# Attention heads taken in pairs on the two halves of TensorE, in a two-block model kernel

## The reference

```
def stick_breaking(q, k, v):          # 8 heads, strictly causal
        z = jnp.einsum('bhqd,bhsd->bhqs', qi, kt) * scale
        log_beta = jax.nn.log_sigmoid(z)
        log_stay = jnp.where(mask, log_beta - z, 0.0)
        log_w = log_beta + lax.cumsum(log_stay, axis=3, reverse=True) - log_stay
        w = jnp.where(mask, jnp.exp(log_w), 0.0)
        return jnp.einsum('bhqs,bhsd->bhqd', w, vt)

def retention(q, k, v, positions):    # 8 heads; q and k turned by rotary()
    scores = jnp.einsum('bnihd,bnjhd->bnhij', qc, kc) * decay_intra
    y_intra = jnp.einsum('bnhij,bnjhd->bnihd', scores, vc)
    ...
```

## Time and profile before

| | us |
|---|---|
| median of 3 runs | 1219.01 (1217.12 to 1223.62) |
| the profiled execution's own time | 1221.8 |
| its span | 1219.7 |
| PE busy | 1046.9 (86%) |
| DVE busy | 887.2 (73%) |
| ACT busy | 438.0 (36%) |
| mean granted clock of TensorE | 0.944 of 2.4 GHz |

### The profile page before, as it was taken

How to read it: one execution, slowest core, us unless ns; L and a number is a source line. 1 busy time by engine, 2 the same in 40 slices (tenths; PEclk the granted TensorE clock), 3 DMA queues, 4 the chain that set the end, 5 groups by cost and what they waited for, 6 DMA issues and landing times.

```text
span 1219.7 us, 14397 instructions
## 1 busy us (share of the span) xinstructions
PE 1046.9 (86%) x5140; PEld 727.9 (60%) x5140; DVE 887.2 (73%) x1809; ACT 438.0 (36%) x845; POOL 291.8 (24%) x260
## 2 busy tenths in 40 slices
PE   6999989999989999976989977876687779766987
PEld 6988989999988776974655532332333334322343
DVE  6977679998768774588676877667766776677545
ACT  5646454444365544543232322222212221222112
POOL 0000000000000000013424644443444444434530
PEclk9999999999999999997999989988988899889999
DMA  9432459889808322029999999999999999999995
GB/s 361 179 139 87 139 211 353 317 326 333 290 35 310 114 94 69 2 102 372 419 419 373 422 421 420 422 421 421 421 422 422 420 422 420 422 421 422 422 421 209
DMA packets 67750, 378.59 MB, mean 310 GB/s; under 512 B 7520, under 2 KB 7776, under 8 KB 34912
## 3 DMA queue, kind: packets, MB, share of 16 engines
q0 software_dynamic: 36864, 268.45, 53.1%
q1 hardware_dynamic: 29952, 107.13, 24.1%
q10 hardware_dynamic: 864, 2.10, 0.5%
HBM read 376.61 MB, written 1.05 MB: 310 GB/s over the span
## 4 chain that ended last, share of the span: by engine, by line
PE 34%; DVE 29%; DMA 24%; ACT 7%; issue 5%; POOL 1%; SPq 0%; ACTq 0%; DVEq 0%
DMA ring_sb<-in_peer,idsb 16%; PE pb L839 5%; PE pb L412 5%; PE pb L415 5%; DVE ring_lo L1311 5%; PE pb L842 5%; DMA whi_rows<-in_peer,idsb 4%; PE pb L440 3%; DVE ring_sb L1840 3%; DMA arena<-in_peer,idsb 3%; DVE arena L1579 2%; DMA xn<-in_peer,idsb 2%; ACT whi L878 2%; DVE arena L1783 1%; DVE arena L1778 1%
## 5 line engine op out<-in xcount | busy, mean ns | idle before, releaser
L1903 POOL DMA_INDIRECT ring_sb<-in_peer,idsb x143 | 163.8, 1146 | 743.3 <-DVE idsb L1823 545.0
L412 PE MATMUL pb<-xhi,whi 128*128 128x256 f32 x928 | 241.7, 294 | 5.9 <-ACT whi L878 1.5
L415 PE MATMUL pb<-xlo,whi 128*128 128x256 f32 x928 | 235.2, 287 | 0.9 <-DVE xlo L1753 0.3
L1840 DVE CUSTOM_DVE_ANT_0 ring_sb<-ring_sb,arena 128x1024 f32<-128x1024 f32 x143 | 171.9, 1222 | 83.6 <-DMA ring_sb<-in_peer,idsb 83.6
L839 PE MATMUL pb<-ring_sb,arena 128*128 128x512 f32 x286 | 162.9, 653 | 81.0 <-ACT arena L1252 81.0
L412 PEld LDWEIGHTS pb<-xhi,whi 128*128 128x128 f32 x928 | 179.5, 193 | 12.8 <-issue 9.5
L415 PEld LDWEIGHTS pb<-xlo,whi 128*128 128x128 f32 x928 | 179.4, 193 | 6.6 <-issue 3.9
L1311 DVE TENSOR_TENSOR ring_lo<-ring_sb,whi 128x1024 fp32r<-128x1024 f32 x138 | 161.5, 1219 | 24.5 <-ACT whi L878 24.5
L1247 ACT ACTIVATE arena<-arena 128x4 f32<-128x4 f32 (+1 forms) x70 | 14.4, 205 | 414.5 <-DVE arena L1840 414.5
L842 PE MATMUL pb<-ring_sb,arena 128*128 128x512 f32 x286 | 156.6, 631 | 0.0
L839 PEld LDWEIGHTS pb<-ring_sb,arena 128*128 128x128 f32 x286 | 57.4, 209 | 157.2 <-issue 157.2
(11 more groups left out here) (320 smaller groups left out, 1646.0 us busy)
## 6 DMA issues: line engine op xcount, KB each, us to landing
ring_sb<-in_ada SPq DMA_DIRECT2D x48, 512.0 KB, 5.4
ring_sb<-in_w_gu SPq DMA_DIRECT2D x44, 512.0 KB, 6.7
ring_sb<-in_w_in SPq DMA_DIRECT2D x40, 512.0 KB, 7.5
ring_sb<-in_w_down SPq DMA_DIRECT2D x22, 512.0 KB, 5.8
ring_sb<-in_w_out SPq DMA_DIRECT2D x16, 512.0 KB, 3.5
ring_sb<-in_w_q SPq DMA_DIRECT2D x16, 512.0 KB, 6.2
ring_sb<-in_peer,idsb POOLq DMA_INDIRECT x143, 22.5
ring_sb<-in_w_iv SPq DMA_DIRECT2D x4, 512.0 KB, 15.9
```

Of the source, the lines that this page charges most:

```text
L412: e.matmul(o, hi_w(u)[:, c], xh(k), start=start, stop=False, skip_group_check=skip)
L415: e.matmul(o, hi_w(u)[:, c], xl(k), start=False, stop=False, skip_group_check=skip)
L1840: e.tensor_tensor_reduce(o, o, h2t[tile], 1.0, 0.0, MUL, ADD, aa[:, col:col + 1]).then_inc(*VD.up(("dot", col)))
L1903: e.indirect_dma_start(rows_at[s], None, peer, bass.IndirectOffsetOnAxis(ap=idsb[:, col:col + 1], axis=0)).then_inc(s_row[s], 16)
```

## The change

Heads are taken in pairs. `pair_scores` issues the 256-column product of both heads of a pair, then the 128-column product of both, each into a bank of its own; `pair_out` does the same with the outputs, both heads into one bank, in its two halves of partitions. The pairs stand in gaps between whole pairs of units: `sb_pair(h)` gives the outputs of heads h-4 and h-3, the cumulations of h-2 and h-1 and the logits of h and h+1. Four gaps hold what nine held; the gaps in the middle of the projections rq and rk for heads are gone. `az`, `be` and `st` exist 4 times. The ring of banks has 6 places during this stage and 4 again behind it. ACT and DVE work pair by pair as well. In the retention the scores of heads 0 to 3 stand together, then those of 4 to 7. The number of arithmetic instructions is the same.

```
-        az, be, st = ([arena[:, w9 + (3 * a + i) * 384:w9 + (3 * a + i + 1) * 384] for i in range(3)] for a in range(3))
+        az, be, st = ([arena[:, w9 + (4 * a + i) * 384:w9 + (4 * a + i + 1) * 384] for i in range(4)] for a in range(3))
...
-            ring[0] = [0, 1, 2, 3]
+            ring[0] = [0, 1, 2, 3, 4, 5]
...
-            def head_scores(kT, qT, h, name, until):
-                r, j = 64 * (h % 2), h // 2
-                b = bank(until)
-                where[name] = b
-                e.matmul(pb[b][:, 0:T], kT[r:r + 64, j * T:j * T + 128], qT[r:r + 64, j * T:(j + 1) * T], start=True, stop=True)
-                return e.matmul(pb[b][:, T:T + 128], kT[r:r + 64, j * T + 128:(j + 1) * T], qT[r:r + 64, j * T + 128:(j + 1) * T],
-                                start=True, stop=True)
-
-            def head_out(w, v, h, b):
-                r, o = 64 * (h % 2), (h // 2 % 2) * T
-                e.matmul(pb[b][r:r + 64, o:o + T], v[:, h * 64:(h + 1) * 64], w[:, 0:T], start=True, stop=False, skip_group_check=True)
-                return e.matmul(pb[b][r:r + 64, o + 128:o + T], v[:, 512 + h * 64:512 + (h + 1) * 64], w[:, T:T + 128],
-                                start=False, stop=True, skip_group_check=True)
+            def pair_scores(kT, qT, h, name, st_, until):
+
+                both, j = (h, h + 1), h // 2
+                for g in both:
+                    where[name, g] = bank((st_, (until, g)))
+                for g in both:
+                    r = 64 * (g % 2)
+                    e.matmul(pb[where[name, g]][:, 0:T], kT[r:r + 64, j * T:j * T + 128], qT[r:r + 64, j * T:(j + 1) * T],
+                             start=True, stop=True)
+                return [e.matmul(pb[where[name, g]][:, T:T + 128], kT[64 * (g % 2):64 * (g % 2) + 64, j * T + 128:(j + 1) * T],
+                                 qT[64 * (g % 2):64 * (g % 2) + 64, j * T + 128:(j + 1) * T], start=True, stop=True) for g in both]
+
+            def pair_out(ws, v, h, b):
+
+                o = (h // 2 % 2) * T
+                for i, w in enumerate(ws):
+                    e.matmul(pb[b][64 * i:64 * i + 64, o:o + T], v[:, (h + i) * 64:(h + i + 1) * 64], w[:, 0:T], start=True, stop=False,
+                             skip_group_check=True)
+                return [e.matmul(pb[b][64 * i:64 * i + 64, o + 128:o + T], v[:, 512 + (h + i) * 64:512 + (h + i + 1) * 64], w[:, T:T + 128],
+                                 start=False, stop=True, skip_group_check=True) for i, w in enumerate(ws)]
...
+            def sb_pair(h):
+
+                if h >= 4:
+                    sb_out(h - 4)
+                if 2 <= h <= 8:
+                    sb_weights(h - 2)
+                    sb_weights(h - 1)
+                if h < 8:
+                    sb_logits(h)
...
-            sb_step(0)
-            gemm(U_rq[0:2], ("rq", 0), (AR, ("rq", "raw", 0)), mid=lambda: sb_step(1))
-            sb_step(2)
+            sb_pair(0)
+            gemm(U_rq[0:2], ("rq", 0), (AR, ("rq", "raw", 0)))
+            sb_pair(2)
             gemm(U_rq[2:4], ("rq", 1), (AR, ("rq", "raw", 1)), mid=lambda: rope_turn("rq", 0))
-            sb_step(3)
+            sb_pair(4)
             rope_turn("rq", 1)
-            gemm(U_rk[0:2], ("rk", 0), (AR, ("rk", "raw", 0)), mid=lambda: sb_step(4))
-            sb_step(5)
+            gemm(U_rk[0:2], ("rk", 0), (AR, ("rk", "raw", 0)))
+            sb_pair(6)
             gemm(U_rk[2:4], ("rk", 1), (AR, ("rk", "raw", 1)), mid=lambda: rope_turn("rk", 0))
-            sb_step(6)
+            sb_pair(8)
             rope_turn("rk", 1)
-            sb_step(7)
-            gemm_tok(U_rv, "rv", (AR, "rv"), mid=lambda: sb_step(8))
-            sb_step(9)
+            gemm_tok(U_rv, "rv", (AR, "rv"), mid=lambda: sb_pair(10))
+            ring[0] = [0, 1, 2, 3]
...
-            for h in range(4):
-                ret_scores(h)
-                if h:
-                    ret_out(h - 1)
-                if h == 2:
-                    group_sum(AS, ("o", 0), AS, half(tmp, 0))
+            ret_scores(0)
+            ret_scores(2)
+            group_sum(AS, ("o", 0), AS, half(tmp, 0))
+            ret_out(0)
             gemm(U_rg[0:2], ("rg", 0), (AR, ("rg", 0)), mid=lambda: group_sum(AS, ("o", 1), AS, half(tmp, 1)))
-            for h in range(4, 8):
-                ret_scores(h)
-                ret_out(h - 1)
-                if h == 5:
-                    ret_mean(0)
-            ret_out(7)
+            ret_out(2)
+            ret_scores(4)
+            ret_scores(6)
+            ret_mean(0)
+            ret_out(4)
+            ret_out(6)
...
+            def sb_pair(h):
+                if 2 <= h <= 8:
+                    for g in (h - 2, h - 1):
+                        e.wait_ge(*VS.at(("be2", g)))
+                        e.activation(az[g % 4], be[g % 4], ACT.Exp).then_inc(*AS.up(("w", g)))
+                if h >= 8:
+                    return
+                for g in (h, h + 1):
+                    e.wait_ge(*PS.at(("z", g)))
+                    if h == 0:
+                        e.wait_ge(*VM.at(("red", 1)))
+                    if g >= 4:
+                        e.wait_ge(*PS.at(("out", g - 4)))
+                    e.activation(az[g % 4], pb[where["z", g]][:, 0:384], ACT.Abs, scale=0.125).then_inc(*AS.up(("abs", g)))
+                for g in (h, h + 1):
+                    e.wait_ge(*AS.at(("abs", g)))
+                    e.activation(az[g % 4], az[g % 4], ACT.Exp, scale=-1.0).then_inc(*AS.up(("exp", g)))
+                for g in (h, h + 1):
+                    e.wait_ge(*AS.at(("exp", g)))
+                    e.activation(az[g % 4], az[g % 4], ACT.Ln, bias=c_("one")).then_inc(*AS.up(("ln", g)))
...
+                for g in (h, h + 1):
+                    e.wait_ge(*PS.at(("cum", g)))
+                    e.tensor_tensor(be[g % 4], be[g % 4], pb[where["cum", g]][:, 0:384], ADD).then_inc(*VS.up(("be2", g)))
+
+            def sb_masks(h):
+                for g in (h, h + 1):
+                    e.wait_ge(*AS.at(("w", g)))
+                    e.tensor_tensor(diag(az[g % 4]), diag(az[g % 4]), sbm, MUL).then_inc(*VS.up(("w", g)))
+
+            def sb_pair(h):
+                if 2 <= h <= 8:
+                    sb_weights(h - 2)
+                    sb_masks(h - 2)
+                if h >= 8:
+                    return
+                for g in (h, h + 1):
+                    p = pb[where["z", g]][:, 0:384]
+                    e.wait_ge(*AS.at(("abs", g)))
+                    if g >= 4:
+                        e.wait_ge(*AS.at(("w", g - 4)))
+                    e.tensor_scalar(be[g % 4], p, 0.125, 0.0, MUL, MIN).then_inc(*VS.up(("be0", g)))
+                for g in (h, h + 1):
+                    m, p = g % 4, pb[where["z", g]][:, 0:384]
+                    e.wait_ge(*VS.at(("be0", g)))
+                    e.wait_ge(*AS.at(("ln", g)))
+                    e.tensor_tensor(be[m], be[m], az[m], SUB).then_inc(*VS.up(("be1", g)))
+                    e.wait_ge(*VS.at(("be1", g)))
+                    if g >= 4:
+                        e.wait_ge(*PS.at(("cum", g - 4)))
+                    e.scalar_tensor_tensor(out=st[m], in0=p, scalar=-0.125, in1=be[m], op0=MUL, op1=ADD).then_inc(*VS.up(("st0", g)))
+                    e.wait_ge(*VS.at(("st0", g)))
+                    e.tensor_tensor(diag(st[m]), diag(st[m]), sbm, MUL).then_inc(*VS.up(("st", g)))
```

More of the change, by code:

```diff
@@ L690, in sb_logits @@
                     e.wait_ge(*VS.at(("k", 1)))
-                head_scores(sbk, sbq, h, ("z", h), (VS, ("st0", h))).then_inc(*PS.up(("z", h)))
+                for g, mm in zip((h, h + 1), pair_scores(sbk, sbq, h, "z", VS, "st0")):
+                    mm.then_inc(*PS.up(("z", g)))
             def sb_weights(h):
-                n = h % 3
+                n = h % 4
                 b = bank((VS, ("be2", h)))
@@ L708, in sb_out @@
                 e.wait_ge(*VS.at(("w", h)))
[L709 to L717, removed]
+                e.wait_ge(*VS.at(("w", h + 1)))
+                for g, mm in zip((h, h + 1), pair_out([az[h % 4], az[(h + 1) % 4]], sv, h, 6 + h // 4)):
+                    mm.then_inc(*PS.up(("out", g)))
+            def sb_pair(h):
[6 more added lines that the diff above has]
+                    sb_logits(h)
             def rope_turn(name, i):
@@ L750, in ret_scores @@
                         e.wait_ge(*VR.at(("rk", "out", i)))
-                head_scores(rk2, rq2, h, ("rs", h), (VR, ("sc", h))).then_inc(*PR.up(("rs", h)))
+                for g, mm in zip((h, h + 1), pair_scores(rk2, rq2, h, "rs", VR, "sc")):
+                    mm.then_inc(*PR.up(("rs", g)))
             def ret_out(h):
@@ L759, in ret_out @@
                 e.wait_ge(*VR.at(("sc", h)))
-                head_out(scR[h % 4], rv, h, 4 + h // 4).then_inc(*PR.up(("out", h)))
+                e.wait_ge(*VR.at(("sc", h + 1)))
+                for g, mm in zip((h, h + 1), pair_out([scR[h % 4], scR[(h + 1) % 4]], rv, h, 4 + h // 4)):
```

(56 more changed lines are left out.)

26 lines of the change are left out of this document (removed).

## The result

| | before | changed | ratio, 95% interval |
|---|---|---|---|
| median, seven runs of each | 1219.01 us (1217.12 to 1223.62) | 1206.93 us (1202.25 to 1210.53) | 0.9885 (0.9861 to 0.991) |
| the same, compared again (before 11 runs, changed 6) | 1221.17 us (1217.0 to 1222.91) | 1205.31 us (1203.24 to 1208.72) | 0.9875 (0.9856 to 0.9894) |

The change saves 1.15%, 12.1 us between the medians, and 15.9 us in the second comparison. The forecast was 1206.6 us in a range of 1203.0 to 1213.5: right. Some terms of its sum are off all the same, and partly offset each other; the experiments are about them.

A forecast was written before the change was run, and what follows sets the result against it. PE was taken to bound stick-breaking and retention. Savings of 8.4 and 4.0 us sum to 12.4, taking the median from 1219.0 to 1206.6 us; the range was 1203 to 1210, or 1203 to 1213.5 with rivals 1 and 2.

The forecast's parts named there:

- PE bounds both stretches: Stick-breaking and retention: PE busy 60.6 of 62.5 and 22.5 of 24.1 us, so savings there count one for one.
- Row halves: Logits or scores of two heads overlap on PE's row halves: 0.87 a pair instead of 1.70, 3.3 us less in stick-breaking.
- Column halves: Two heads' outputs overlap fully on PE's column halves: 0.81 a pair, 3.1 us less in stick-breaking, 3.1 in retention.
- The fold: Eight 24-column matmuls on column quarters, all within 0.28 us, at least 0.33 one after another; evidence that columns overlap.
- rival 1: Column halves do not overlap; stick-breaking saves 3.1 less, total gain 7.8, 1211.2 us; chance 0.20.
- The walk through stick-breaking: PE's steps from first logits to rv's end: 8.6 less, including 1.9 of PE idling; 8.4 after a bank wait.
- The bank ahead of rk's second pair: DVE's turn of q's second half frees it at 430.1, PE asks at 430.0; put at 0.2 us.
- Slack of ACT and DVE: Second heads' masked logits in stick-breaking are ready before PE's cumulation asks; slack shrinks to 0.7 us.
- Rivals 2 and 3: 2: ACT or DVE bound last two pairs, gain 9, 1210, chance 0.15; 3: late chains lower PE's clock, 1225.4, 0.03.
- The ring of six: In force from some 50 us before 399; listed waits there not for banks, so 0, bounds minus 0.5 to plus 0.5.
- The walk through the retention: PE's steps from rv's end to the last mean: 20.05 instead of 24.1 us, saving 4.0 of the possible 5.6.
- All that follows is shifted: Work behind the attention starts earlier by what is saved; rest of the span stays 734 us, within 2 us.

The follow-up runs named there:

- the copy on DVE: Changed kernel with one more 128x1024 DVE copy, its result unused, behind each of the four pairs' logits; 1212.96 us (1 run).
- the same half: Changed kernel with both heads' outputs of a pair written to one half of PE's columns; 1207.49 us, ratio to before 0.989.
- heads apart: Changed kernel with stick-breaking work inside each gap taken head by head, retention as changed; 1214.10 us, ratio to before 0.9944.
- the turn on DVE first: Changed kernel with retention reordered to fill waits, and DVE's turn of q's second half ahead of rk's units' rest; 1205.36 us, ratio to before 0.9879.

## Why the prediction was right, point by point

- **PE bounds both stretches.** Right for stick-breaking: 52.74 of 53.12 us busy, and the copy on DVE shows that DVE is as close there as the prediction feared: 1.81 of 2.07 us added ahead of the bank came through. In the retention it holds only in part: 3.4 of 20.4 us are waits.
- **Row halves, 0.87 a pair.** Measured 0.85.
- **Column halves, 0.81 a pair, the nearer end of bounds 0.81 and 1.58.** Measured 0.80; 1.44 with the same half. The fold was the right row to judge by, and rival 1 is refuted. Its price of 3.1 for stick-breaking is that of both effects together, 4 x 0.78; the halves alone are worth 4 x 0.64, of which 2.1 came through (the wait at the bank covered 0.44), and 1.25 in the retention.
- **The walk through stick-breaking, saved 8.4.** S fell by 9.47. The retention's scores start 52.98 behind the first logits, where 53.9 was given (54.1 with the bank's 0.2, which that figure leaves out). The mis-sized term is two cumulations at 2 x 1.06: the four lots took 1.83, 1.93, 1.93 and 1.84, 0.95 less than 8.48 in all. 1.06 is the time of one that stands between two products on halves of the array; with whole-array work on both sides it is 0.87 (404.15 to 405.02), with it on one side 0.96 (405.02 to 405.98, or 402.36 to 403.32 with heads apart). Side by side, a pair has two such borders or one, where two single ones had four.
- **The bank ahead of rk's second pair, 0.2.** 0.38 idle; the turn on DVE first takes 0.44 off S.
- **Slack of ACT and DVE.** DVE ends the second heads' masks earlier than carried through. From DVE's timeline of the changed kernel:

```profile
412.48 0.42 DVE L1677 TENSOR_TENSOR arena<-arena,cs 128x256 f32<-128x256 f32 x1
...
423.96 0.42 DVE L1677 TENSOR_TENSOR arena<-arena,cs 128x256 f32<-128x256 f32 x1
...
427.30 0.69 DVE L1684 TENSOR_TENSOR sq<-pb,sinT 128x512 f32<-128x512 f32 x1
...
435.10 0.42 DVE L1677 TENSOR_TENSOR arena<-arena,cs 128x256 f32<-128x256 f32 x1
```

  The ends are 412.9, 424.4 and 435.5; the second cumulations start at 415.4, 425.8 and 436.6. Slack 2.5, 1.4 and 1.1, where 2.5, 1.7 (1.6 by the walk's own times) and 0.7 were given. Rivals 2 and 3 did not come: no PE row waits at line 706. The row of 427.30 ends at 427.99, and PE's wait at 428.04 is for it.
- **The ring of six, taken at 0 with bounds of half a us.** This step failed. In before, four banks cost 0.65 ahead of the first logits, in sight as the wait of 0.57 at 399.02: it names a copy, and what PE needed was the bank that the copy frees. With heads in pairs they would cost 1.13 there (1.33 against 0.20) and 2.1 within S. The latter was in the sum under another name: I had let "the 1.9 us that PE idles now" go without saying what makes it go. Widening the ring alone removes it (62.45 to 60.59).
- **The walk through the retention, 20.05.** Measured 20.37, saved 3.7 instead of 4.0. The waits that were forecast came in their size, 0.70 ahead of the first group sum included. What was missing is small: the walk let PE go on when ACT's square ends, and each time it goes on 0.14 later. From ACT's timeline of the changed kernel:

```profile
452.20 0.63 ACT L1105 ACTIVATE sq<-xn 128x512 f32<-128x512 f32 x1
...
457.93 0.63 ACT L1105 ACTIVATE sq<-xn 128x512 f32<-128x512 f32 x1
```

  The ends are 452.83 and 458.56, the sums start at 452.97 and 458.70: 0.28 of the 0.32.
- **All that follows is shifted.** Rest 734.15 and 734.31. Right.

In sum 13.8 us, not 12.4: 0.95 and 0.65 under-counted, 0.3 over-counted, and small change. The median moved by 12.1, in the second comparison by 15.9, the profiled execution by 14.1. Against runs that spread by 8 us this difference is none, so that the median came out as forecast is partly luck.

## What to carry to other kernels

Where two products use different halves of the rows or of the columns of the matrix engine, issue them next to each other: here, with 256 and 128 columns each, a pair cost what one did, in either order inside it. Before giving a wait to the engine that is named, ask which bank or buffer that engine's instruction frees; two more banks removed four waits, 2.3 us, from the kernel before, and none of them was named as a bank's. When work is moved out of a place, list what ran beside it there: if it stood in the shadow of a neighbour's copy, moving it gains nothing there, and the wait comes to light. And a delay can cost more than its own length: behind 2.19 us of idle time the clock took another 1.5.

## What was not expected of the hardware

- Each change between products on the whole array and products on a half of it costs about 0.1 us: a cumulation takes 0.87, 0.96 or 1.06 with none, one or two such borders. The Trainium skill, "TensorEngine Tiling (Array Packing)", section "Key Properties", says that a change of the tiling mode drains the engine; the 0.1 us agree with a cost of such a change, but no row shows that a drain is what makes it.
- The copy of 128x1024 on DVE took 0.69 us, where the subtraction of the same size (line 1311 of before, 2.35 for two) takes 1.2. By the Trainium skill, "VectorE: DVE Perf Modes", section "Mode 2×_2P — use both read ports for one tensor", an operation with one source may read with both ports, one with two sources may not; the two durations agree with that.
